# The first of eleven projection blocks of the attention, moved ahead of the barrier between the delta stage and the attention stage

## The reference

```
p = x @ w_in                       # one projection, its columns split among the heads
A: gated DeltaNet, 8 heads of 128: causal conv, l2 norms, delta rule in chunks, gated rms norm
B: sparse attention, 16 query heads of 64, 2 kv heads: compressed, selected and window branches
h = sigmoid(gA) * o_A + sigmoid(gB) * o_B
x = LayerNorm(alpha * x + h @ w_out)
x = LayerNorm(alpha * x + MoE(x))  # 64 SwiGLU experts, top 6, and a shared one
```

## Time and profile before

| | |
|---|---|
| median of 3 runs | 1845.7 us (1844.94 to 1845.77) |
| profiled execution, its own time | 1835.2 us |
| its span | 1833.4 us |
| mean granted TensorE clock | 0.976 of full |
| TensorE matmuls busy | 94% of the span |

### The profile page before, as it was taken

How to read it: one execution, slowest core, us unless ns; L and a number is a source line. 1 busy time by engine, 2 the same in 40 slices (tenths; PEclk the granted TensorE clock), 3 DMA queues, 4 the chain that set the end, 5 groups by cost and what they waited for, 6 DMA issues and landing times. The chain is left out here.

```text
span 1833.4 us, 26633 instructions
## 1 busy us (share of the span) xinstructions
PE 1722.8 (94%) x10063; PEld 1148.6 (63%) x10063; DVE 794.4 (43%) x1929; ACT 523.8 (29%) x1248; POOL 337.2 (18%) x352
## 2 busy tenths in 40 slices
PE   8999999999999989899888999999998998999986
PEld 6687777877877868788666765575444444444432
DVE  1154664664664410265888653472222222222216
ACT  2224234234233220365676543111111111111110
POOL 0011210211211120131554551001111111111100
PEclk9999999999999989799799999999999999999999
DMA  8071221221232252152100564978999999999988
GB/s 244 1 227 45 71 73 49 66 78 49 60 84 48 47 166 55 48 176 84 36 2 1 181 219 153 359 324 340 375 420 420 419 421 420 419 420 420 419 349 321
DMA packets 168543, 371.70 MB, mean 203 GB/s; under 512 B 36903, under 2 KB 114719, under 8 KB 143584
## 3 DMA queue, kind: packets, MB, share of 16 engines
q1 hardware_dynamic: 148208, 308.69, 45.7%
q0 software_dynamic: 19728, 60.06, 9.2%
q10 hardware_dynamic: 480, 1.25, 0.2%
HBM read 337.75 MB, written 48.15 MB: 210 GB/s over the span
## 5 line engine op out<-in xcount | busy, mean ns | idle before, releaser
L861 PE MATMUL bank<-xT,arena 128*128 128x272 f32 x1440 | 368.2, 399 | 0.0
L861 PEld LDWEIGHTS bank<-xT,arena 128*128 128x128 f32 x1440 | 259.8, 190 | 62.3 <-issue 16.3
L2874 PE MATMUL bank<-arena,kvt 128*64 128x512 f32 (+1 forms) x816 | 256.1, 610 | 21.6 <-issue 20.7
L2874 PEld LDWEIGHTS bank<-arena,kvt 128*64 128x64 f32 (+1 forms) x816 | 88.1, 148 | 151.5 <-issue 151.5
L2971 PE MATMUL bank<-arena,kvt 128*64 128x512 f32 (+1 forms) x408 | 127.8, 598 | 2.2 <-issue 2.1
L3297 DVE SCALAR_TENSOR_TENSOR kvt<-kvt,arena,bank 128x256 f32<-128x256 f32 x37 | 17.8, 481 | 239.0 <-ACT kvt L3079 239.0
L1291 POOL TENSOR_TENSOR arena<-arena 128x512 f32<-128x512 f32 x40 | 46.3, 1157 | 381.5 <-DVE arena L1382 257.0
L2874 PE MATMUL bank<-xT,kvt 128*64 128x512 f32 (+1 forms) x208 | 97.0, 622 | 9.3 <-issue 9.3
L2711 POOL DMA_INDIRECT hT<-x_rows,rows_i x37 | 37.5, 1014 | 350.9 <-DVE rows_i L3232 328.9
L3079 ACT ACTIVATE kvt<-bank 128x256 f32<-128x256 f32 x37 | 14.2, 383 | 276.9 <-PE bank L2874 276.9
L1657 PE MATMUL bank<-xT,arena 128*128 128x272 f32 x352 | 83.4, 401 | 8.6 <-PEq L168 8.6
(11 more groups left out here) (519 smaller groups left out, 2960.3 us busy)
## 6 DMA issues: line engine op xcount, KB each, us to landing
arena<-in_w_exp_gate SPq DMA_DIRECT2D x51, 1024.0 KB, 22.5
arena<-in_w_exp_up SPq DMA_DIRECT2D x51, 1024.0 KB, 25.5
arena<-in_w_exp_down SPq DMA_DIRECT2D x51, 1024.0 KB, 23.8
arena<-in_w_in SPq DMA_DIRECT2D x48, 512.0 KB, 5.5
kvt<-in_w_exp_down SPq DMA_DIRECT2D x13, 1024.0 KB, 23.1
xT<-in_w_exp_gate SPq DMA_DIRECT2D x13, 1024.0 KB, 21.6
xT<-in_w_exp_up SPq DMA_DIRECT2D x13, 1024.0 KB, 25.0
y_rows<-arena SPq DMA_DIRECT2D x1, 12800.0 KB, 39.9
```

Source lines behind the costliest of these rows:

```text
L861: last = mm(banks[2 * (i % 2) + half][:, 0:HALF], wh[blk % RING][:, k, :], xT[:, k, half * HALF:(half + 1) * HALF], start=(k == 0), stop=( ...
L2874: last = mm(banks[2 + 4 * (t % 2)][cols, :], xgT[:, k, cols], ewgu[i % EBUF][:, :, k], start=(k == 0), stop=(k == KD - 1))
```

## The change

The first of the eleven attention blocks (number 45) is made in the delta stage, by TensorE, right behind `output_sums()`, into banks 2 and 3. Its waits are for its weights and for the copy of unit 51 out of those banks. In the attention stage TensorE's loop begins at n = 1 and the banks are swapped, so that block 1 uses banks 0 and 1. ScalarE copies block 0 out as its first act in the attention stage, without a wait. The load of block 6, into the slot of block 0, needs no wait any more; `prj_banked` counts one less throughout.

```diff
--- before.py
+++ after.py
@@ -1048,6 +1048,13 @@
             sample_sums(2, 3)
             output_sums()
 
+            pe.wait_ge(wh_in[FIRST_ATT % RING], landed_by(FIRST_ATT))
+            pe.wait_ge(pr_saved, unit_of(H, 3) + 1)
+            for half in range(2):
+                for k in range(KD):
+                    mm(banks[2 + half][:, 0:HALF], wh[FIRST_ATT % RING][:, k, :], xT[:, k, half * HALF:(half + 1) * HALF],
+                       start=(k == 0), stop=(k == KD - 1))
+
 
         @block.scalar
         def _(sc):
@@ -1591,9 +1598,10 @@
             for a in range(4):
                 sp.dma_start(page_p[32 * a:32 * a + 32], rows[a]).then_inc(rows_p_in, 16)
             for p in range(RING, ATT_BLOCKS):
-                sp.wait_ge(prj_banked, p - RING + 1)
+                if p > RING:
+                    sp.wait_ge(prj_banked, p - RING)
                 load_attention(sp, p, wh_in)
-            sp.wait_ge(prj_banked, ATT_BLOCKS)
+            sp.wait_ge(prj_banked, ATT_BLOCKS - 1)
             sp.dma_start(pos_rows[0:32], io["nsa_cmp_pos"][0].rearrange("s (m u) d -> (s m) (u d)", u=2)).then_inc(c2_in, 16)
             w2 = io["nsa_cmp_w2"][0]
             for dst, n in ((W2k[0:HD], 0), (W2v[0:HD], 1)):
@@ -1646,7 +1654,7 @@
         def _(pe):
             mm, tr = nc.tensor.matmul, nc.tensor.transpose
 
-            for n in range(ATT_BLOCKS):
+            for n in range(1, ATT_BLOCKS):
                 blk = FIRST_ATT + n
                 if n >= RING:
                     pe.wait_ge(wh_in[blk % RING], 16)
@@ -1654,7 +1662,7 @@
                     pe.wait_ge(prj_saved, n - 1)
                 for half in range(2):
                     for k in range(KD):
-                        last = mm(banks[2 * (n % 2) + half][:, 0:HALF], wh[blk % RING][:, k, :],
+                        last = mm(banks[2 * ((n + 1) % 2) + half][:, 0:HALF], wh[blk % RING][:, k, :],
                                   xT[:, k, half * HALF:(half + 1) * HALF], start=(k == 0), stop=(k == KD - 1))
                 last.then_inc(prj_banked, 1)
             pe.wait_ge(prj_saved, ATT_BLOCKS)
@@ -1992,10 +2000,11 @@
             step = Steps(sc, act_step)
 
             for n in range(ATT_BLOCKS):
-                sc.wait_ge(prj_banked, n + 1)
+                if n >= 1:
+                    sc.wait_ge(prj_banked, n)
                 dst = qT[:, NQ_AHEAD[n]] if n < len(NQ_AHEAD) else mgB[:, n - len(NQ_AHEAD)]
                 for half in range(2):
-                    last = actv(dst[:, half * HALF:(half + 1) * HALF], banks[2 * (n % 2) + half][:, 0:HALF], ACT.Copy)
+                    last = actv(dst[:, half * HALF:(half + 1) * HALF], banks[2 * ((n + 1) % 2) + half][:, 0:HALF], ACT.Copy)
                 last.then_inc(prj_saved, 1)
 
             sc.wait_ge(prj_saved, ATT_BLOCKS)
```

## The result

The changed kernel took 1835.3 us (median of 5 runs, 1831.1 to 1836.9) and the kernel before 1845.4 us (5 runs, 1844.9 to 1845.8): ratio 0.9941, 95% interval 0.9927 to 0.9956, that is 10.1 us or 0.6% faster. Two more sets of runs gave 0.9957 (0.9944 to 0.9970) and 0.9952 (0.9939 to 0.9965). The forecast was 1836.2 us.

The account below looks back on a forecast made before the run. TensorE, busy 94% of the span, idles 8.59 us at the barrier before attention and restarts at half clock. 7.33 + 2.54 - 0.39 = 9.48 us off 1845.7 gives 1836.2 us, range 1832.8 to 1840.5 (8 in 10).

Parts of the forecast that it names:

- The block taken out: Attention stage: sixteen matmuls fewer between the barrier and the last save, a gain of 7.33 us.
- The cover: End of delta stage: head 7's tail on other engines hides the moved block; without it the block costs 7.33 us again.
- The barrier: Between delta and attention stages: TensorE now comes last, so attention starts 0.39 us later; bounds 0 to 1.0 us.
- The clock: First projections behind the barrier: TensorE's short pause keeps the clock up, a gain of 2.54 us; bounds 0 and 2.54.
- Saves, loads, gathers at nothing: Attention stage: ScalarE's save of block 0 and the earlier load of block 6 beside the gathers cost nothing.
- Carried to the end: Behind the projections: later work hangs on semaphores, not fixed times, so the whole 9.48 us reaches the end.
- The offset of 10.5 us between the profiled execution and the median: Whole kernel: the timed median lies 10.5 us above the profiled execution's 1835.2; the same gain was subtracted from the median.
- the clock falls at the barrier all the same: Rival, at the barrier: the clock still drops, leaving a gain of 7.0 to 7.8 us, 1837.9 to 1838.7; chance 9%.
- slower through the clock later on: Rival, later in attention: more clock falls, 1.7 us each, lose over 9.5 us; with six, 1846.4 us; chance 2%.

Follow-up runs that it names:

- third set: Kernel before, changed kernel, warm only and uncovered run side by side; before 1842.4 us, changed 1833.4 us, ratio 0.9952.
- warm only: Kernel before, with block 45 made once more behind the output sums, unread, all eleven still made later; 1835.1 us, ratio 0.9981; again 1839.7 us, 0.9991.
- half a block: Kernel before, with only half of block 45 (8 matmuls) moved behind the output sums; 1831.2 us, ratio 0.9961; again 1840.4 us, 0.9991.
- uncovered: Changed kernel, with the moved block ahead of the last sums instead of behind them; 1835.1 us, ratio 0.9986 against before; again 1842.0 us, 1.0003.
- held-back load: Changed kernel, with the load of block 6 waiting until block 1 has been made; 1833.9 us, 0.4 us from the changed kernel.
- two blocks: Changed kernel, with block 46 also made ahead of the barrier, into banks 0 and 1; 1835.2 us, ratio 0.9968 against before.

## Why the prediction was right, step by step

The terms, each as measured below, add up to what the profiles show: 7.33 + 2.5 - 0.14 = 9.7 us for the first pair, which shows 9.70 up to the tanh, and 7.33 + 2.9 - 0.13 = 10.1 for the pair of the third set, which shows 10.09; forecast 9.48.

- **The block taken out, 7.33 us.** Right. Changed against warm only differs in just this (and the earlier load, which costs nothing): sums to tanh 91.49 - 84.16 = 7.33, in the third set's medians 6.3 us. The block made in the delta stage took its 7.49 us of records without a wait; both waits were free, as forecast.
- **The cover.** Right: with the block ahead of the sums the gain fell from 8.6 to 0.0 us in the third set (2.4 us left in the first). The mere shortening of the attention stage gives nothing that these runs show; the 2.1 to 2.5 us kept up to the tanh are the shorter tail and the shorter slow stretch.
- **The barrier, 0.39 us.** Right in kind, too large. TensorE does end 0.37 us after VectorE, but the stretch from the sums to the first matmul grew from 9.70 to 9.83 or 9.84 us only: 0.13. I had taken the 1.65 us behind TensorE from the earlier trace rows; here it is 1.39 or 1.40, in all six profiles where this one block comes last. The trace's records of the sequencers, which the timeline leaves out, show where the 0.26 lie. At the next barrier the last matmul ends at 1145.66 and raises a semaphore (`first_banked`) that the program lets TensorE wait for (`pe.wait_ge(first_banked, 1)`, the last line of its stream); only then, at 1145.95, is TensorE's part in the barrier done, 0.29 us behind the end. The moved block has no such signal and no such wait: it ends at 665.14, and TensorE's part is done at 665.17. VectorE, which waits for its own last instruction too, takes 0.27 us (665.37 to 665.64 in the profile before). From there on all three take the same 1.36 to 1.37 us to the first matmul. The 1.65 us of rows 6 thus held 0.26 us of waiting that the moved block doesn't have; and TensorE's part is done 0.13 us after VectorE's (665.17 and 665.04), which is the whole loss.
- **The clock, 2.54 us.** Right in kind and, for the profile before, in size: warm only gains 2.5 us up to the tanh with no work removed. But it varies. From the first matmul behind the barrier to the last save, less the blocks' 7.33 us each and 0.23 of lag (by the profiles at full clock it is 0.23 to 0.3), the low clock cost 2.5 us in the first profile before, 2.7 and 2.9 in the two others, 2.8 and 3.05 with half a block, 1.5 and 1.6 in the two of uncovered. The trace's record of the clock gives the same: in the three profiles of before it was back at full 5.06, 5.40 and 5.85 us after TensorE's restart, at 672.07, 672.47 and 673.34, and half of that is lost at 0.50. The Trainium skill ("TensorE: Matmul & The Clock Gate", Part 1, "What's actually happening") says that the count of slow matmuls differs from run to run; these profiles agree in that: 2.5 to 2.9 us in three of one and the same kernel, 1.5 to 3.05 over all. The step that the prediction drew from it, to leave the term out, would have been wrong here: with the long pause the term was never nothing, and the sum without it, 1838.8, is further off than the sum with it.
- **Saves, loads, gathers at nothing.** Right, within what the runs can tell: the held-back load changed 0.4 us, and the saves keep their 7.33.
- **Carried to the end.** Right on the mean of the sets: 10.1, 8.5 and 8.6 us against 9.7 to 10.1 up to the tanh. A microsecond may be given back behind it; the intervals are about 2.5 us to either side and don't decide. That the forecast lay within 0.9 us of the median, closer than these intervals reach, is in part luck.
- **The offset of 10.5 us between the profiled execution and the median.** I carried it along unexplained. Most of it is placed now, against the kernel's profile in the third set, whose span is 11.0 us longer (1844.4): 5.7 us are the stretch from the first window-cache load, 92.0 us against 97.7, and 4.2 are the third stage, 686.1 against 690.3. Why either differs is open.

The rival "the clock falls at the barrier all the same" did not come true in the three profiles of the changed kernel, nor in those of warm only and of the held-back load, but two blocks, with 0.7 us more of pause, showed how near it was. The trace of before had rows of pauses between 1.79 and 3.06 us, which the prediction says it lacked: one of 2.42 us at 1355.39, with the clock at 0.75 from there to 1361, and one of 2.43 at 1459.84, with 1.00 up to 1466. At such a length it goes either way. The rival "slower through the clock later on" did not appear: from 770 to 1010 us the mean clock is 0.93 in the three profiles of before and 0.94 to 0.95 in the four of the changed kernel and the held-back load.

## What to carry to other kernels

Ahead of a barrier, look for the engine that comes first: independent work from behind the barrier can be laid into its wait, up to about the length of the others' tail (here 7.33 us into 6.94) and no further, and its results must be able to rest in banks that nobody needs until the other side. If that engine is TensorE, a pause like these of 4.9 us and more costs twice, once as time and once as the slow stretch behind it; both go together. And before subtracting two traces, ask whether each comes from an execution that took what its kernel usually takes; compare stretches that start at the same event, and profile the kernel before again beside the new one.

## What the runs showed that I had not expected

In the sets with the longer stretch, VectorE and ScalarE start some instructions 3 to 5 us after the matmuls that they wait for have ended, with no other release in the profile. The same instruction in the first profile before and in the one after:

```profile
1028.44 0.42 DVE L2352 TENSOR_TENSOR arena<-bank,arena 128x256 f32<-128x256 f32 x1 [1.04 <-PE bank L1805]
```

```profile
1021.17 0.42 DVE L2361 TENSOR_TENSOR arena<-bank,arena 128x256 f32<-128x256 f32 x1 [4.79 <-remote]
```

The waits listed as "remote" stand in none of the five profiles with the stretch of 92.0 us, and in all of the nine with the longer one: one of 3.2 to 4.8 us on VectorE, two of about 3.1 on ScalarE (in the first profile after, two more of 3.0 on VectorE). GpSimd is issuing gathers at these places in both kinds. The trace's semaphore records show that the signal itself comes late: behind the matmul of L1805, whose record ends at 1028.41 in the first profile, the semaphore rises at 1028.42; in the one after the matmul ends at 1017.37 and the semaphore rises at 1021.15. At this place it is 2.2 to 3.8 us late in all nine profiles and on time in all five. I have no run that tells what holds the signal back, or why it goes with the set; it is open.
